# A fused decoder trunk: a piece of the memory-key product moved between the first attention scores, and half of the probability weighting moved to ScalarE

## The reference

```python
s = jnp.einsum('bqgrd,bngd->bgrqn', qb, kc).astype(jnp.float32) * scale
p_c = masked_softmax(s, cmp_end[None, :] <= t[:, None])
o_c = jnp.einsum('bgrqn,bngd->bqgrd', p_c.astype(qb.dtype), vc)
...
return gb[..., 0:1] * o_c + gb[..., 1:2] * o_s + gb[..., 2:3] * o_w
...
kv = mem @ wkv
k = kv[..., :D].reshape(B, M, X_HEADS, X_HEAD_DIM)
v = kv[..., D:].reshape(B, M, X_HEADS, X_HEAD_DIM)
```

## Time and profile before

| | us |
|---|---|
| median of 3 runs | 1497.58 |
| the runs | 1496.54 to 1499.34 |
| profiled execution, its own time | 1497.81 |
| its span, first to last instruction | 1496.0 |

### The profile page before, as it was taken

The page is one execution under the profiler, slowest core; times in us unless marked ns, Lnnn a source line. Parts: engine busy times, 40 slices in busy tenths (PEclk is TensorE's granted clock), DMA queues, the critical chain, the costliest instruction groups (busy, mean ns, idle before and its releaser), DMA issues.

```text
span 1496.0 us, 21243 instructions
## 1 busy us (share of the span) xinstructions
PE 1473.7 (99%) x7766; PEld 1237.3 (83%) x7766; DVE 561.1 (38%) x944; ACT 608.6 (41%) x1225; POOL 668.7 (45%) x530
## 2 busy tenths in 40 slices
PE   8999999999999999999999999999999999999998
PEld 7889888888898888888888867788888888888886
DVE  2753784744561011100114488664443011101014
ACT  3345664354343233322224388635433333323221
POOL 5542224342574444454456525543153444454442
PEclk9999999999999999999999999999999999999999
DMA  9331113321353333332233512333133333332232
GB/s 243 98 95 60 37 47 124 102 87 42 100 167 92 100 97 98 91 101 97 99 113 114 150 54 82 129 100 99 36 104 105 103 95 95 91 105 96 94 99 91
DMA packets 115713, 147.04 MB, mean 98 GB/s; under 512 B 20534, under 2 KB 74160, under 8 KB 115632
## 3 DMA queue, kind: packets, MB, share of 16 engines
q1 hardware_dynamic: 115312, 145.87, 32.1%
q0 software_dynamic: 320, 0.08, 0.0%
HBM read 143.80 MB, written 2.10 MB: 98 GB/s over the span
## 4 chain that ended last, share of the span: by engine, by line
PE 91%; ACT 3%; DVE 3%; issue 1%; POOL 1%; DMA 0%; SPq 0%; DVEq 0%; ACTq 0%
PE ps L659 82%; PE ps L664 4%; PE ps L898 1%; PE ps L853 1%; POOL w_lo L622 1%; DVE h L1776 1%; DMA x_res<-in_x 0%; PE ps L817 0%; DVE h L1750 0%; PE ps L849 0%; ACT w_hi L1094 0%; PE ps L950 0%; DVE ib L1767 0%; DVE y_lo L1466 0%; DVE h L1783 0%
## 5 line engine op out<-in xcount | busy, mean ns | idle before, releaser
L622 POOL TENSOR_TENSOR w_lo<-w_raw,w_hi 128x512 fp32r<-128x512 f32 (+2 forms) x468 | 603.0, 1298 | 798.3 <-ACT w_hi L1094 796.7
L1094 ACT ACTIVATE w_hi<-w_raw 128x512 fp32r<-128x512 f32 (+2 forms) x468 | 280.4, 614 | 540.5 <-PE ps L659 521.5
L659 PE MATMUL ps<-fm_hi,w_hi 128*128 128x512 f32 (+1 forms) x1112 | 421.6, 379 | 4.2 <-POOL w_lo L622 2.5
L659 PE MATMUL ps<-fm_lo,w_hi 128*128 128x512 f32 (+1 forms) x1112 | 419.2, 377 | 0.0
L659 PE MATMUL ps<-fm_hi,w_lo 128*128 128x512 f32 (+1 forms) x1112 | 419.1, 377 | 0.0
L659 PEld LDWEIGHTS ps<-fm_hi,w_hi 128*128 128x128 f32 x1112 | 209.2, 188 | 45.6 <-POOL w_lo L622 3.9
L659 PEld LDWEIGHTS ps<-fm_hi,w_lo 128*128 128x128 f32 x1112 | 209.2, 188 | 38.9
L659 PEld LDWEIGHTS ps<-fm_lo,w_hi 128*128 128x128 f32 x1112 | 209.2, 188 | 38.2 <-issue 0.5
L1914 DVE TENSOR_TENSOR gf<-silu,ps 128x512 f32<-128x512 f32 x44 | 28.3, 684 | 414.7 <-ACT silu L1433 397.6
L1658 DVE SCALAR_TENSOR_TENSOR x_res<-x_res,ps 128x512 f32<-128x512 f32 x48 | 31.4, 685 | 273.5 <-PE ps L659 188.2
L659 PE MATMUL ps<-w_hi,g_hi 128*128 128x512 f32 x288 | 112.0, 389 | 0.0
(11 more groups left out here) (279 smaller groups left out, 2168.7 us busy)
## 6 DMA issues: line engine op xcount, KB each, us to landing
w_raw<-in_f_w_up SPq DMA_DIRECT2D x352, 128.0 KB, 2.1
w_raw<-in_f_w_down SPq DMA_DIRECT2D x88, 256.0 KB, 2.6
w_raw<-in_x_wkv SPq DMA_DIRECT2D x48, 256.0 KB, 3.1
w_raw<-in_o_w_in SPq DMA_DIRECT2D x40, 256.0 KB, 2.6
w_raw<-in_x_wq SPq DMA_DIRECT2D x32, 256.0 KB, 2.7
w_raw<-in_x_wo SPq DMA_DIRECT2D x32, 256.0 KB, 2.8
w_raw<-in_e_w_in SPq DMA_DIRECT2D x24, 256.0 KB, 3.2
w_raw<-in_o_w_out SPq DMA_DIRECT2D x20, 256.0 KB, 2.7
```

The lines of the kernel that those rows point to most:

```text
L622: nc.gpsimd.tensor_tensor(lo[:, :n], w_raw[:, c % RING, :n], hi[:, :n].bitcast(F32), ALU.subtract).then_inc(w_split, 1)
L659: last = nc.tensor.matmul(outp, lhsT, rhs, start=(clear and k == 0 and n == 0), stop=(k == steps - 1 and n == 2), skip_group_check=True)
L1094: nc.scalar.activation(w_pair(c)[0][:, :n], w_raw[:, s, :n], ACT.Copy).then_inc(w_rounded, 1)
```

## The change

It has two parts. The first moves the last three chunks of `k0_1` on TensorE from ahead of `scores(0)` to between `scores(0)` and `scores(1)`, and turns the compressed keys (`tkc`) three chunks earlier. ScalarE takes `exps(0)` ahead of the evacuation of `k0_1`, and VectorE takes `weigh_probs(0)` ahead of `row_max(1)`. The second gives the weighting of the second half of each unit's heads to ScalarE (`weigh_half`), for all units but the four of `cmp`. VectorE signals that the weights are there (`weights_ready`), and `weighted` becomes two semaphores.

```diff
+def weighted_by(u):
+    halves = [(2, 0) if b == "cmp" else (1, 1) for _, b, _, _ in UNITS[:u + 1]]
+    return sum(d for d, _ in halves), sum(s for _, s in halves)
...
-            product("k0_1", mem, MEM, True, chunks=(0, KT - 1))
+            product("k0_1", mem, MEM, True, chunks=(0, KT // 2))
             b0 = begin("tkc")
...
-            product("k0_1", mem, MEM, True, chunks=(KT - 1, KT))
+            product("k0_1", mem, MEM, True, chunks=(KT // 2, KT // 2 + 1))
...
                 for j in (0, 1):
-                    pe.wait_ge(weighted, 2 * u + j + 1)
+                    d, s = weighted_by(u)
+                    if UNITS[u][1] == "cmp":
+                        pe.wait_ge(weighted_d, d - 1 + j)
+                    elif j:
+                        pe.wait_ge(weighted_a, s)
+                    else:
+                        pe.wait_ge(weighted_d, d)
...
             scores(0)
+            product("k0_1", mem, MEM, True, chunks=(KT // 2 + 1, KT))
             scores(1)
-            evacuated("k0_1")
             pe.wait_ge(exped, 1)
             scores(2)
+            evacuated("k0_1")
...
-            keys_evac(0, 1)
...
+            def weigh_half(u):
+                if UNITS[u][1] == "cmp":
+                    return
+                heads = UNITS[u][3]
+                act.wait_ge(weights_ready, u + 1)
+                for r in range(heads // 2, heads):
+                    p = probs_of(u, r)
+                    last = nc.scalar.activation(p, p, ACT.Copy, scale=weight[:, u % 2, r:r + 1])
+                last.then_inc(weighted_a, 1)
...
             exps(0)
+            keys_evac(0, 1)
             exps(1)
...
                 turned_copy(u)
+                if u + 1 < len(UNITS):
+                    weigh_half(u + 1)
                 for n in range(filled_until(u - 2) // KT, filled_until(u - 1) // KT):
                     values_filled(n)
...
+                    nc.vector.tensor_tensor(wt, wt, gt, ALU.mult).then_inc(weights_ready, 1)
+                    dve.wait_ge(weights_ready, u + 1)
+                    for r in range(heads // 2):
+                        p = probs_of(u, r)
+                        last = nc.vector.tensor_scalar(p, p, weight[:, u % 2, r:r + 1], None, ALU.mult)
+                    last.then_inc(weighted_d, 1)
...
             row_max(0)
+            weigh_probs(0)
             row_max(1)
-            weigh_probs(0)
             row_max(2)
```

More of the change, by code:

```diff
@@ L366, in hybrid_trunk @@
         vc_cleared = sem("vc_cleared")
-        weighted, copied_d, copied_a = sem("weighted"), sem("copied_d"), sem("copied_a")
+        weights_ready, weighted_d, weighted_a = sem("weights_ready"), sem("weighted_d"), sem("weighted_a")
+        copied_d, copied_a = sem("copied_d"), sem("copied_a")
         pv_done, o_hi_ready, o_ready = sem("pv_done"), sem("o_hi_ready"), sem("o_ready")
@@ L1612, in weigh_probs @@
                 gt = gates[:, qb, h0 * 3:(h0 + heads) * 3].rearrange("p (r c) -> p r c", c=3)[:, :, GATE_OF[b]]
-                settle(nc.vector.tensor_tensor(wt, wt, gt, ALU.mult))
                 if b == "cmp":
[L1615 to L1626, removed]
+                    settle(nc.vector.tensor_tensor(wt, wt, gt, ALU.mult))
+                    nc.vector.tensor_scalar(wt, wt, consts[:, C_ROWOK + qb:C_ROWOK + qb + 1], None, ALU.mult).then_inc(weights_ready, 1)
+                    dve.wait_ge(weights_ready, u + 1)
+                    for r0 in (0, GROUP):
+                        p = probs[:, u % 2, 32 * r0:32 * (r0 + GROUP)].rearrange("p (r n) -> p r n", n=32)[:, :, 0:NCMP]
+                        w = weight[:, u % 2, r0:r0 + GROUP].unsqueeze(2).to_broadcast([P, GROUP, NCMP])
+                        nc.vector.tensor_tensor(p, p, w, ALU.mult).then_inc(weighted_d, 1)
+                else:
+                    nc.vector.tensor_tensor(wt, wt, gt, ALU.mult).then_inc(weights_ready, 1)
+                    dve.wait_ge(weights_ready, u + 1)
+                    for r in range(heads // 2):
+                        p = probs_of(u, r)
+                        last = nc.vector.tensor_scalar(p, p, weight[:, u % 2, r:r + 1], None, ALU.mult)
+                    last.then_inc(weighted_d, 1)
             def turned_half(u):
```

## The result

| | us |
|---|---|
| before, median (range) | 1497.58 (1495.95 to 1499.34) |
| changed, median of 15 runs (range) | 1502.3 (1500.77 to 1503.97) |
| ratio, 95% interval | 1.003 (1.0023 to 1.0037) |
| span of the profiled execution | 1500.3 (before 1496.0) |

The change makes the kernel 0.3% slower, 4.7 us by the medians and 4.3 us by the two profiled spans. The forecast was 1500.9 in a range of 1498.4 to 1502.9.

The account below looks back on a forecast made before the run. TensorE, busy 1473.7 of 1496.0 us, was taken to bound the kernel. Forecast: 1497.8 + 0 (keys) + 0 (clock) + 0 (VectorE) + 3.1 (ScalarE) = 1500.9 us; own range 1499.9 to 1502, whole range 1498.4 to 1502.9.

Parts of the forecast that it names:

- The keys, worth 0 in waits: Start of attention: two TensorE gaps become one of about 1.7 us before scores(3); gain on the path 0.
- the chain named there: Start: scores(1), VectorE's row maximum of unit 1, ScalarE's exponentials, then scores(3); exponentials end at 146.5, scores(3) starts at 146.55.
- The clock, taken as 0: Start: the clock falls again to 0.51 for some 3.5 us, difference 0, with -1.7 us as the other end.
- VectorE, worth 0: Attention: 32 of 64 weighting instructions leave VectorE; none ends a wait of a matmul, so 0 us.
- ScalarE's six terms, 3.1 us: Attention: 32 new ScalarE instructions mostly fit its waiting, but delay TensorE at six places, 3.1 us in all.
- unit 2: Round of unit 1: its weighting delays the exponentials of unit 3, so scores(5) starts later, +0.6 us.
- unit 7, with the values behind it: Rounds of units 6 and 7: weighting delays unit 8's exponentials and scores(10); the 0.29 memory-value wait vanishes behind; +0.5 us.
- unit 9: Rounds of units 8 and 9: ScalarE waits for VectorE's weights, so unit 10's exponentials and scores(12) come later, +0.3 us.
- unit 13: Round of unit 13: waiting for weights, then weighting unit 14, delays the copy of the memory values, +0.6 us.
- unit 16: Round of unit 15: its weighting with its wait delays unit 17's exponentials ahead of scores(19), +0.4 us.
- unit 19: Round of unit 19: the third copy of memory values, with 512 columns, comes later, +0.7 us.
- a second fall of the clock: Rival: clock falls again at the 0.8 us wait of unit 6's round or unit 13's; +1.7 us, 1502.6; chance 0.14.

Follow-up runs that it names:

- the first part: Only the changed order of keys, exponentials and weights at the start, VectorE weighting all heads, against the kernel before: 1499.23 us, ratio 1.0009.
- the second part alone: ScalarE weights the second half of the heads, the start as in the kernel before, against that kernel: 1500.55 us, ratio 1.002.

## Why the prediction was right

**What bounds.** Right. Half of VectorE's weighting was taken away and nothing came back on any path; ScalarE, with 34.3 us to spare in all, made TensorE wait in the few rounds that had less. The 1.6 us that the prediction gives per round are per place of waiting, of which there were 21; over the 26 rounds it is 1.3. Nothing in the sum hangs on it.

**The keys, worth 0 in waits.** Right: one gap of 1.84 us for two of 0.92 and 0.78, and from the start of scores(1) to that of scores(3) it is 6.60 us in both kernels. Before and changed:

```profile
139.95 0.59 PE L843 MATMUL ps<-causal_b,ident_b 128*128 128x512 bf16 x2
```

```profile
140.25 0.61 PE L851 MATMUL ps<-causal_b,ident_b 128*128 128x512 bf16 x2
```

The experiment with the chunks one place later shows that the chain named there was the one that bound.

**The clock, taken as 0.** This is the one term that was mis-sized. It fell, as forecast, but in the profile it stayed at half speed for 6.8 us and not 3.4. In the medians the first part costs 1.8 us. I had bounded this term by a gain only, and took the length of the slow stretch from before as given, though its length varies from run to run by steps worth 1.6 us.

The page "TensorE: Matmul & The Clock Gate" of the Trainium skill (section "HAM oscillation — how this bites in real kernels"), weighed in the prediction, puts the loss down to longer idle gaps, and this case disagrees again: with a gap of 1.82 to 1.84 us the clock fell in all five profiles that have it and, by the groups of its times, in every run of the first part. With no gap at this place (the keys behind scores(1)) the clock held in the profile and, by the times, in 8 of 11 runs.

**VectorE, worth 0.** Right as far as the starts show: between the places of the table below they never move back by more than 0.04 us.

**ScalarE's six terms, 3.1 us.** By the second part alone, 3.1. Place by place, from how the starts moved in the changed kernel:

| | predicted | measured |
|---|---|---|
| unit 2 | 0.6 | some 0.2 behind the slow clock; waits of 0.49 and 0.96 with the clock back sooner |
| unit 7, with the values behind it | 0.5 | 0.5 (2.02 just ahead of scores(10), 2.53 at the values) |
| unit 9 | 0.3 | 0.15 (2.53 to 2.68) |
| unit 13 | 0.6 | 0.66 (to 3.34) |
| unit 16 | 0.4 | 0.44 (to 3.78) |
| unit 19 | 0.7 | 0.67 (to 4.45) |

So in the profile of the change the terms add up to 2.6, and the rest of the 4.45 is about 1.6 of clock and the 0.30 by which scores(1) already started later (139.95 to 140.25), whose source no run singles out. At unit 9 VectorE's weights, 0.47 us long in the earlier trace rows, took 0.16 here:

```profile
185.01 0.16 DVE L1650 TENSOR_TENSOR weight<-weight,gates 128x2 f32<-128x2 f32 x1
```

**The price of the new instructions.** They were a little longer than the exponentials taken for them: 390, 502, 618 and 724 ns for 128 to 512 columns, against 378, 476, 583 and 688.

```profile
L1223 ACT ACTIVATE probs<-probs,weight 128x512 f32<-128x512 f32 x8 | 5.8, 724 | 0.9 <-DVE weight L1650 0.9
...
L1223 ACT ACTIVATE probs<-probs,weight 128x384 f32<-128x384 f32 x8 | 4.9, 618 | 1.1 <-DVE weight L1650 0.9
...
L1223 ACT ACTIVATE probs<-probs,weight 128x256 f32<-128x256 f32 x8 | 3.6, 502 | 0.9 <-DVE weight L1650 0.9
L1223 ACT ACTIVATE probs<-probs,weight 128x128 f32<-128x128 f32 x8 | 2.5, 390 | 0.3 <-DVE weight L1650 0.3
```

**The rivals.** None came true. The nearest was a second fall of the clock by 1.7 us: its size was right, but it didn't come at the waits of units 7 or 13 (0.71 and 0.85 us, with the clock at 1.00 from 155.2 us on); it lengthened the first. I had put the merged gap down as a possible help to the clock, and it was the opposite.

**The range.** The forecast's own range, 1499.9 to 1502, doesn't hold the measured 1502.3. The whole range does, because it was stretched to 1502.9 for a second fall of the clock at other places, which didn't come. That the time lies inside is in part luck: the terms of ScalarE came out near the sum (3.1 us by themselves, 2.6 in the profile of the change), and what lies above the forecast is for the most part the clock term.

## What to carry to other kernels

Work that is to hide a wait has to stand behind the instruction that starts the awaited chain. The three chunks ahead of scores(1) hid nothing, one place later they hid all of it, which with the clock was worth 3.2 us.

An engine with much idle time in the mean can still be the wrong place for more work: go through the rounds one by one, take the slack of each, and look at what stands behind the new instruction and at what the new instruction itself waits for. Take the loss from how the start of the same instruction moves between two traces, not from the gap in brackets.

## What the runs showed of the hardware

With two short idle gaps of TensorE (0.92 and 0.78 us) the profiles of the kernel before and of the second part alone have 3.4 us at half clock. With one gap of 1.82 to 1.84 us four of five profiles have 6.8 us and one has 3.4, though TensorE had work all through it. With no gap at this place, in the other three profiles, there is no half clock in the attention at all. The work in the slow stretch of the change is scores of 31 columns, six products of 256, values products and transposes of 128, and from 154.3 us scores of 256; what in it kept the clock low wasn't tried.

A gap by itself is not enough: the whole change with the keys behind scores(1) waits 0.96 us before scores(5), longer than either gap of the kernel before, and the clock stays at 1.00; behind that gap come scores and products of 256 columns, ahead of it stand values products and transposes of 128.

The times of one kernel fall into groups 1.6 us apart, and how many runs fall into which differs between the kernels with two gaps, with one and with none at this place. Two single executions of one kernel can differ by 1.6 us in this way, as 1496.0 and 1497.6 do here.
